# Two-block transformer, one core: experts of the token stages are ranked and paired fullest with emptiest, and the first block's experts gather in halves

## The reference

```python
g_idx = argmax(xf @ w_grp + b_grp)                 # one group of eight experts per token
top_l, top_e = top_k(in_grp, 2)                    # two experts inside it
y[token] = sum over the two of gate * (silu(x Wg[e]) * (x Wu[e])) @ Wd[e]   # Wg, Wu: 1024x512, Wd: 512x1024
```

## Time and profile before

| what | value |
|---|---|
| device time, median of 3 runs | 3010.57 us (3005.5 to 3010.97) |
| device time of the profiled execution | 3005.34 us |
| its span | 3003.5 us |
| TensorE busy | 2590.0 us, 86% |
| first block's experts, first gate matmul to end of last values | 632 to 1155 us |
| token stage, first layer, first expert matmul to last store | 1527 to 2000 us |
| laps of the first layer, to the first indirect gather | 2000 to 2070 us |
| token stage, second layer | 2484 to 2960 us |

### The profile page before, as it was taken

The page is one execution under the profiler, slowest core; times in us unless marked ns, Lnnn a source line. Parts: engine busy times, 40 slices in busy tenths (PEclk is TensorE's granted clock), DMA queues, the critical chain, the costliest instruction groups (busy, mean ns, idle before and its releaser), DMA issues. The chain is left out here.

```text
span 3003.5 us, 42120 instructions
## 1 busy us (share of the span) xinstructions
PE 2590.0 (86%) x17577; PEld 1342.1 (45%) x17577; DVE 875.0 (29%) x1831; ACT 623.2 (21%) x1213; POOL 238.4 (8%) x213
## 2 busy tenths in 40 slices
PE   6998788869999999998989988874998789898983
PEld 3544676533334334445444444432346644434441
DVE  2654573221121121456430000003333651000002
ACT  4412342310001011332111111103223321101112
POOL 0100443100000000001100000001002320000001
PEclk8999898889999999999989999997999989999997
DMA  8231202549999983001569999995203228999995
GB/s 319 85 129 68 73 4 87 190 205 422 415 413 415 398 346 123 22 1 56 188 273 423 429 428 429 428 383 191 106 1 131 91 85 327 428 427 427 427 428 239
DMA packets 109840, 755.40 MB, mean 252 GB/s; under 512 B 20980, under 2 KB 24416, under 8 KB 70768
## 3 DMA queue, kind: packets, MB, share of 16 engines
q1 hardware_dynamic: 106224, 738.38, 60.0%
q0 software_dynamic: 2592, 12.58, 1.1%
q10 hardware_dynamic: 864, 2.10, 0.2%
HBM read 727.07 MB, written 25.97 MB: 251 GB/s over the span
## 5 line engine op out<-in xcount | busy, mean ns | idle before, releaser
L1973 PE MATMUL bank<-ring,expert_in 128*64 128x512 f32 x1536 | 338.9, 595 | 25.1 <-DMA ring<-in_moe_w_up_dram 21.4
L1908 DVE TENSOR_TENSOR hidden<-silu_gate,bank 128x512 f32<-128x512 f32 x32 | 33.8, 1057 | 737.8 <-PE bank L1973 737.8
L1702 PE MATMUL bank<-ring,expert_in 128*64 128x512 f32 x1024 | 224.8, 597 | 7.8 <-DVE home L1550 5.5
L1973 PEld LDWEIGHTS bank<-ring,expert_in 128*64 128x64 f32 x1536 | 120.8, 137 | 237.4 <-issue 234.7
L1984 PE MATMUL bank<-ring,hidden_T 128*64 128x512 f32 x768 | 170.1, 595 | 31.8 <-ACT hidden_T L1932 31.8
L1962 PEld LDWEIGHTS bank<-onehot,x_part 128*128 128x128 bf16 x3072 | 175.1, 99 | 29.1 <-issue 24.3
L1962 PE MATMUL bank<-onehot,x_part 128*128 128x128 bf16 x3072 | 180.6, 221 | 4.6 <-DVE onehot L1899 4.6
L1702 PEld LDWEIGHTS bank<-ring,expert_in 128*64 128x64 f32 x1024 | 73.3, 138 | 157.0 <-issue 141.7
L1717 PE MATMUL bank<-ring,hidden_T 128*64 128x512 f32 x512 | 122.6, 641 | 3.8 <-ACT hidden_T L1625 3.8
L2699 PE MATMUL bank<-ring,home 128*128 128x512 f32 x256 | 119.6, 629 | 3.6 <-PEq L205 3.6
L621 PE MATMUL bank<-home,ring 128*128 128x512 f32 (+1 forms) x320 | 114.6, 518 | 6.2 <-PEq L205 6.2
(11 more groups left out here) (653 smaller groups left out, 3682.5 us busy)
## 6 DMA issues: line engine op xcount, KB each, us to landing
ring<-in_moe_w_gate_dram SPq DMA_DIRECT2D x52, 2048.0 KB, 20.7
ring<-in_moe_w_up_dram SPq DMA_DIRECT2D x50, 2048.0 KB, 25.5
ring<-in_moe_w_down_dram SPq DMA_DIRECT2D x50, 2048.0 KB, 26.9
ring<-in_w_gate_dram SPq DMA_DIRECT2D x32, 2048.0 KB, 13.1
ring<-in_w_up_dram SPq DMA_DIRECT2D x32, 2048.0 KB, 14.4
ring<-in_w_down_dram SPq DMA_DIRECT2D x32, 2048.0 KB, 16.0
ring<-in_w_mod_dram SPq DMA_DIRECT2D x12, 2048.0 KB, 10.2
home<-in_moe_w_down_dram SPq DMA_DIRECT2D x9, 2048.0 KB, 28.5
```

What stands on the lines that cost most here:

```text
L1702: mm = pe.matmul(B[2 + 2 * part + b][rows, :], xe[:, dc, rows], ws[e][:, c, b * COLS:(b + 1) * COLS], start=(dc == 0), stop=(dc == NC - 1))
L1973: mm = pe.matmul(B[2 + 2 * part][rows, :], xe[:, c, rows], ws[e][:, c, :], start=(c == 0), stop=(c == NC - 1))
```

## The change

1. In the token stages VectorE ranks experts 4 to 31 by their counts (`places_of_experts`, new, called before `rows_of_choices`). Experts 0 to 3 keep their places (`FIXED`). The three fullest are paired with the three emptiest in pairs 5, 6 and 7, counted from 0 (`FIRST_UNEVEN`, `UNEVEN`); there the full expert has 96 columns (`MANY`) and the empty one 32 (`FEW`). The counts that decide on laps are shifted to match.
2. In these three pairs `into_hidden` and `down` issue four matmuls of 32 columns where two of 64 were: three for the full expert, one for the empty one.
3. From pair 2 on SP and VectorE read the experts' numbers from memory (`value_load` of `who`), SP after a wait on `places_known`. TensorE's instructions of the 16 pairs are written out without a loop.
4. In the first block's experts the gather is cut in two halves of four chunks. TensorE now does `turn_onehot`, the half into bank 1, the transposes, the half into bank 0, `down`; ScalarE does `turned` and the hidden copy before `inputs`. The up matmuls go bank by bank over two chunks, so that the first of them waits for seven additions and the first on the other bank for the eighth.
5. In the gated linear attention VectorE makes the two tables from others that are resident; their load is dropped.

```diff
+FIXED = 4
+UNEVEN = 3
+FIRST_UNEVEN = 5
+MANY, FEW = 3 * SLOTS // 2, SLOTS // 2
...
-                        inputs(x + 1)
+                        turned(x + 1, 1 - parity)
...
+                def gather(x, half):
+                    if half:
+                        pe.wait_ge(onehot_ready, x + 1)
+                    else:
+                        pe.wait_ge(onehot_T_ready, x + 1)
+                    for c in range(4 * half, 4 * half + 4):
                         k = 0
                         for part in range(3):
                             for t in range(NT):
                                 mm = pe.matmul(B[c // 4][:, c % 4 * P:(c % 4 + 1) * P], src[part][:, t, c * P:(c + 1) * P],
                                                oh[:, t, :], start=(k == 0), stop=(k == 3 * NT - 1))
                                 k += 1
-                    mm.then_inc(gathered, 1)
+                    if half == 0:
+                        mm.then_inc(gathered, 1)
 
                 def turn_onehot(x):
-                    pe.wait_ge(input_ready, x + 1)
+                    pe.wait_ge(onehot_ready, x + 1)
+                    wait(pe, input_ready, x)
...
-                        for c in range(chunks):
+                        for at, b, more in itertools.product(range(0, chunks, 2), range(NB), range(2)):
+                            c = at + more
                             dc = l * chunks + c
-                            for b in range(NB):
-                                for e in range(2):
-                                    rows = slice(e * SLOTS, (e + 1) * SLOTS)
-                                    mm = pe.matmul(B[2 + 2 * part + b][rows, :], xe[:, dc, rows], ws[e][:, c, b * COLS:(b + 1) * COLS],
-                                                   start=(dc == 0), stop=(dc == NC - 1))
-                                    if c == chunks - 1 and b == NB - 1:
-                                        mm.then_inc(m.weights_used, 1)
+                            if part and dc == 0:
+                                wait(pe, added, 8 * x - 1 + b)
+                            for e in range(2):
+                                rows = slice(e * SLOTS, (e + 1) * SLOTS)
+                                mm = pe.matmul(B[2 + 2 * part + b][rows, :], xe[:, dc, rows], ws[e][:, c, b * COLS:(b + 1) * COLS],
+                                               start=(dc == 0), stop=(dc == NC - 1))
+                                if c == chunks - 1 and b == NB - 1:
+                                    mm.then_inc(m.weights_used, 1)
...
-                        pe.wait_ge(added, 8 * x)
                     into_hidden(x, 1)
                     more = not isinstance(x, int) or x < pairs - 1
                     if more:
-                        gather(x + 1)
+                        turn_onehot(x + 1)
+                        gather(x + 1, 1)
                     pe.wait_ge(hidden_ready, x + 1)
                     for c in range(NF):
                         mm = pe.transpose(B[2 + c // 4][:, c % 4 * P:(c % 4 + 1) * P], hid[:, c * P:(c + 1) * P], m.c("ident"))
                     mm.then_inc(hidden_turned, 1)
                     if more:
-                        turn_onehot(x + 1)
+                        gather(x + 1, 0)
...
+                def experts_at(x):
+
+                    at = [slice(2 * x + e, 2 * x + e + 1) if isinstance(x, int) else bass.ds(2 * x + e, 1) for e in range(2)]
+                    return [sp.value_load(who[0:1, a], min_val=0, max_val=E - 1) for a in at]
+
+                def issue(g, r, qs):
+
+                    if r < 2:
+                        parts = [l for _, l in pair_loads(wg, wu, wd, r)]
+                    else:
+                        two = [expert_loads(wg, wu, wd, e) for e in experts_at(r if isinstance(g, int) else 4 * g + r)]
+                        parts = [l for both in zip(*two) for l in both]
+                    for q in qs:
+                        k = loads * r + q
+                        sp.wait_ge(m.weights_used, (k if isinstance(g, int) else 4 * loads * g + k) + (base - WIDE + 1))
+                        src_w, chunks, cols = parts[q]
+                        dst, arrived, _ = home(k, chunks, cols)
+                        sp.dma_start(dst, src_w).then_inc(arrived, 16)
...
+                sp.wait_ge(places_known, 1)
                 with sp.Fori(0, (pairs - 4) // 4) as g:
                     for r in range(2, 6):
-                        for q in range(loads):
-                            issue(g, r, q)
+                        issue(g, r, range(loads))
...
+                    if isinstance(x, int) and x < FIXED // 2:
+                        dve.tensor_copy(at_pair[:, :, :], pos[:, 2 * x:2 * x + 2, :]).then_inc(slots_copied, 1)
+                    else:
+                        for e in range(2):
+                            at = slice(2 * x + e, 2 * x + e + 1) if isinstance(x, int) else bass.ds(2 * x + e, 1)
+                            one = dve.value_load(who[0:1, at], min_val=0, max_val=E - 1)
+                            ins = dve.tensor_copy(at_pair[:, e:e + 1, :], pos[:, bass.ds(one, 1), :])
+                        ins.then_inc(slots_copied, 1)
                     dve.wait_ge(slots_copied, x + 1)
                     for t in range(NT):
-                        ins = dve.tensor_tensor(oh[:, t, :, :], lane, at_pair[:, :, t:t + 1].to_broadcast([P, 2, SLOTS]), ALU.is_equal)
+                        if is_uneven(x):
+                            flat = oh[:, t, :, :].rearrange("p e s -> p (e s)")
+                            for e, cut in enumerate((slice(0, MANY), slice(MANY, P))):
+                                ins = dve.tensor_tensor(flat[:, cut], lane_uneven[:, cut], at_pair[:, e, t:t + 1].to_broadcast([P, cut.stop - cut.start]), ALU.is_equal)
+                        else:
+                            ins = dve.tensor_tensor(oh[:, t, :, :], lane, at_pair[:, :, t:t + 1].to_broadcast([P, 2, SLOTS]), ALU.is_equal)
...
+                order = Order(dve, choice_order)
+                places_of_experts(dve, order, places_known, E, R, K, who)
+                dve.tensor_scalar(lane_uneven[:, SLOTS:MANY], R.lane[:, 0:FEW], float(SLOTS), None, ALU.add)
+                dve.tensor_copy(lane_uneven[:, 0:SLOTS], R.lane[:, 0:SLOTS])
+                order.then(dve.tensor_copy(lane_uneven[:, MANY:], R.lane[:, 0:FEW]))
+                rows_of_choices(dve, order, laps_known, E, R, Q, K[-1])
+                dve.wait_ge(places_known, 1)
+                pair(0)
+                for x in range(1, FIRST_UNEVEN + UNEVEN - 1):
+                    pair(x)
+                with dve.Fori(FIRST_UNEVEN + UNEVEN - 1, pairs - 1) as x:
+                    pair(x)
+                pair(pairs - 1)
...
+                even = [(0, slice(0, SLOTS), True), (1, slice(SLOTS, P), True)]
+                uneven = [(0, slice(0, FEW), False), (0, slice(FEW, 2 * FEW), False), (0, slice(2 * FEW, MANY), True), (1, slice(MANY, P), True)]
+                strips_of = lambda g, r: uneven if isinstance(g, int) and is_uneven(r) else even
+
                 def into_hidden(g, r, part):
 
                     ws = [slot(g, r, part * third + e) for e in range(2)]
                     for c in range(NC):
-                        for e in range(2):
-                            rows = slice(e * SLOTS, (e + 1) * SLOTS)
+                        for e, rows, ends in strips_of(g, r):
                             mm = pe.matmul(B[2 + 2 * part][rows, :], xe[:, c, rows], ws[e][:, c, :],
                                            start=(c == 0), stop=(c == NC - 1))
-                            if c == NC - 1:
+                            if c == NC - 1 and ends:
                                 mm.then_inc(m.weights_used, 1)
 
                 def down(g, r):
                     ws = [slot(g, r, 2 * third + e) for e in range(2)]
                     for c in range(NF):
                         for b in range(2):
-                            for e in range(2):
-                                rows = slice(e * SLOTS, (e + 1) * SLOTS)
+                            for e, rows, ends in strips_of(g, r):
                                 mm = pe.matmul(B[6 + b][rows, :], hT[:, c, rows], ws[e][:, c, b * COLS:(b + 1) * COLS],
                                                start=(c == 0), stop=(c == NF - 1))
-                                if c == NF - 1 and b == 1:
+                                if c == NF - 1 and b == 1 and ends:
                                     mm.then_inc(m.weights_used, 1)
...
-                pair(0, 0)
-                with pe.Fori(0, (pairs - 4) // 4) as g:
-                    for r in range(1, 5):
-                        pair(g, r)
-                for r in range(pairs - 3, pairs):
+                for r in range(pairs):
                     pair(0, r)
...
+def places_of_experts(dve, order, places_known, E, R, K, who):
+
+    key, pairs, rank, heavy, light, step, place, shift, base = K
```

(34 more changed lines are left out.)

52 lines of the change are left out of this document (23 added, 29 removed).

## The result

The changed kernel took 2935.26 us (median of 4 executions, 2928.92 to 2939.52) against 3010.58: ratio 0.976, 95% interval 0.9748 to 0.9773. The forecast was 2935. The profiled execution took 2933.97 us, its span is 2932.2, so 71.3 us went from one profiled span to the other. The two ways of counting differ: the medians lie 75.3 us apart, the profiles 71.3, and the forecast's sum is 75.2.

The account below looks back on a forecast made before the run. Transfers bound the token stages, waits for slots and TensorE the first block's later experts. Gains of 59.5 + 12 + 2 + 1.7 = 75.2 us from 3010.6 gave 2935.4, predicted 2935 us, range 2922 to 2955.

Parts of the forecast that it names:

- What bounds the stages: Token stages take what their bytes take, at 427 GB/s; TensorE's work matters there only where it outgrows the transfers.
- Laps of the first layer: Between first token stage and next gather: laps go from three to zero, 59.5 us gained, bounds 57 and 61.
- First block's experts: First block's expert stage: pairs fall from 61.3 to 59.1 us, bound by weight loads; 12 us gained, bounds 0 and 17.
- Four strips: Uneven token-stage pairs: 32-column groups run side by side, 0.3 us more TensorE time per pair, hidden by transfers: 0.
- Ranking on VectorE: Start of token stages: the longer VectorE chain is covered by 6 us of slack: 0, bound 3 us for both.
- Loads by number: Token stages: SP and VectorE reading expert numbers ahead of loads and one-hots costs 0, bounded by 6 us.
- TensorE without a loop: Token stages: two loop waits, 15.5 us together, are mostly hidden by transfers; 2 us gained, bounds 0 and 4.
- sum of bounds at worst: All terms at their worst: 57 + 0 + 0 + 1 - 3 = 55 us gained, 2955 us.
- The prediction's rival: Both loop waits lie on the path, so 15.5 us come back and not 2: 2922 us, chance 0.03.
- Tables: Linear attention: two VectorE instructions replace the table load TensorE waits 3.3 us for; 1.7 us gained, bounds 1 and 2.5.

Follow-up runs that it names:

- even pairs: The changed kernel with 64 columns for every expert, so three overflow laps of the first layer come back: 2997.97 us.
- strips everywhere: The changed kernel with four strips of 32 columns in all 16 pairs of both token stages: 2936.17 us.
- TensorE's lap code out: The changed kernel with TensorE's code for the overflow laps left out and the other engines' lap code kept: 2924.89 us.
- stores by ScalarE: The changed kernel with the stores of the experts' rows issued by ScalarE behind its own copies, none by SyncE: 2932.66 us.
- numbers early: The changed kernel with SyncE reading the expert numbers of the third to sixth pair ahead of the store: 2932.25 us.
- no lap code, no such load: The changed kernel without the lap stage and without the load of the first lap's gate weights: 2915.74 us, ratio 0.9699.
- the version that joined ScalarE's stores to other edits: The changed kernel with lap code ending each engine's token-stage program, stores by ScalarE, and TensorE's lap branch ahead of the last three pairs: 2919.06 us.

## Why the prediction was right, and where it was not

- *What bounds the stages.* Right. Token stages lie between 447.3 and 451.8 us through even pairs, strips everywhere and a changed queue, with 426 to 428 GB/s in every window behind the first pair.
- *Laps of the first layer.* Right in mechanism, 1.3 us too large: 58.2 for 59.5. The term took off 1.5 us for what may come back; it was 12.0 - 9.2 = 2.8 us at the gather, and 0.6 more up to the first scaled row (7.6 us behind the gather, 6.95 before). Named as cause were the first lap's gate weights, and the profiles bear that out, by another way than the working had. They do not hold up the barrier behind the lap stage; the token stage's last store lands behind them. First layer, us from the store's issue:

  | profile | gate weights landed | store landed | next transfer |
  |---|---|---|---|
  | changed kernel | 4.0 | 5.3 | 11.3 |
  | TensorE's lap code out | 3.0 | 4.1 | 6.8 |
  | stores by ScalarE | 2.5 | 3.8 | 10.0 |
  | numbers early | 2.3 | 3.5 | 9.7 |
  | strips everywhere | 0.7 | 2.7 | 8.8 |
  | no lap code, no such load | none | 2.7 | 3.5 |

  With the same lap code the gap falls from 11.3 to 8.8 us as the weights land earlier, and store to gather is then 9.6 us in the first layer and 9.3 in the second: the excess is gone with the load still there. No run took out the load alone. The working compared the two layers and so took the second's 9.2 us as a floor; it was no floor: 5.6 us of it were the empty lap stage. (It also counts 18.9 MB of weights as gone; the first gate load stays, so it is 16.8.)
- *First block's experts.* Right: 12.7 for 12. From up to up five pairs take 295.3 us, 59.06 each, against a forecast of 59.1 from the bytes; `down` at 13.95 us and a share of 1.01 are as forecast too. The prediction did not separate the halves from the order by bank; the run did.
- *Four strips.* Right: 7.07 us for 64 instructions is 0.44 us a group of four.
- *Ranking on VectorE.* Right: the chain's last row ends at 1517.75, and the second one-hots are ready at 1518.9, 6.4 us ahead of `hidden`, for a forecast slack of 6.
- *Loads by number.* Nearly: the read shows as a share of 0.89 in the first 28 us, which the prediction had listed as a sign that it would be wrong, but its cost is 0 to 1.4 us, inside the bound of 6. (That bound is missing from the sum of bounds at worst: with it the end is 2962 us and not 2955.)
- *TensorE without a loop.* The term that failed. It gave 2 us with bounds 0 and 4; alone it is 3 to 9 us slower, of which the token stages show 1.4; the rest lies in code that no edit touched, and whether the lower clock there comes from the edit is open. The waits lay behind transfers as argued, stage 2 gained 2.1 and 1.0 us, but stage 1 lost 3.5 and 2.9, which no bound allowed. (The prediction's rival calls each wait longer than a double load; 7.8 us is longer than one load of 4.9, and shorter than two.) What makes stage 1 longer is known in part: more data between the cuts, 0.2 MB of it instructions, and in the changed kernel 1.7 us of idle transfers in the first 28 us (0.89 for 0.95). The rest is open: the stage is 447.3 us in both profiles of kernels with the loop, and 450.2 to 451.8 in ten of the twelve others; the two exceptions are 448.8 (numbers early) and 447.7 (ScalarE's stores), and the version that joined ScalarE's stores to other edits was at 451.0 again. The Trainium skill (Runtime: NRT & Kernel Launch, "Instruction fetch mechanics") says that a taken branch out of the fetched window stalls its engine while the target page is fetched; the trace agrees in place: the instruction queue moves 16 KB inside both loop waits and in the gap of the lap skip. It does not agree at every loop end, since two passes of the first layer fetched nothing and did not wait.
- *Tables.* Right in place: SyncE's first transfer to TensorE's first matmul of that stage fell from 2.19 to 0.47 us, 1.7 less. The stretch as a whole shows 0.3: 0.6 went to the later first row, and the last 0.8 is not placed.
- *The total.* That 2935.26 fell on 2935.4 is luck in part. Between the profiles, on whose rows the sum was made, 71.3 us went and not 75.2, though -3.1 us at the start, which is the clock's, helped. The misses on the other side are +2.9 in stage 1, 1.3 at the laps, 1.4 up to token stage 2, 1.0 in stage 2 and +1.6 at the end. The last is the second layer's last `down`, 8.8 us for 7.1 before, with the granted clock at 0.57 over its first 3.3 us (1.00 before). That the medians lie 75.3 us apart comes from executions that spread over 5 and 11 us.

## What to carry to other kernels

Code that is skipped is not free: a stage in which four engines branched past code that was never run cost 5.2 to 5.6 us here on the path, and next to nothing once the branch stood beside a landing store or where its engine was waiting for transfers. Measure such a gap from the landing of what came before it, not from its issue. Compare a stage with an empty version of itself, not only with its shortest occurrence, before calling the rest a floor. And cut the profiles at equal events: the total moved 11 us by the granted clock, while a stage bound by transfers repeated within 0.2 us.

## What the runs showed of the hardware

- Four groups of 32 columns ran side by side also where two or three of them share the moving weights: 64 instructions in 7.07 us, 32 of 64 columns in 7.09.
- A stage that only skips lap code in four engines costs 5.2 us in one layer and 5.6 in the other, counted from the landing of the last store, TensorE's skip 3.3 and 3.8 of it; the same skip three pairs earlier shows as 3.3 us.
- A 512 KB store issued while a 2 MB load was still on its way landed 1.1 to 1.3 us behind that load: 5.3, 4.1, 3.8 and 3.5 us after its issue, against 2.7 where the load had landed 0.7 us behind the store's issue or was left out.
- A loop of TensorE over four pairs fetched no instructions in two passes of the first layer, and fetched them anew in each pass of the second, with a wait of 7.8 us at two of the loop's ends.
- Reading two numbers of experts put SyncE's next loads 2.7 us behind a store, where they followed after 0.7 before the change.
- In executions of one kernel, the one before the change, on more than one chip, the granted clock over the whole went from 0.935 to 0.941 and the time from 3012.7 to 2999.3 us.
